# The value product of an attention stage: three passes per key tile against a half-empty stationary operand, or two passes against a full one, with the halves added afterwards

## What is computed

```python
for l in range(DEPTH):
    h = modulate(x, norm_mix_g[l], shift, scale)
    q, k, v = mixer_inputs(h, w_in[l], ...)      # 16 heads: 4 neighbourhood, 6 latent (MLA), 6 grouped (GQA)
    p = softmax(q @ k.T * scale + bias)          # latent queries: 512 latent + 128 cached context keys
    o = p @ v                                    # head dim 64
    x = x + gate_a * (concat(o) @ w_out[l])
    x = x + gate_f * swiglu(modulate(x, ...), w_gate[l], w_up[l], w_down[l])
```

## Time and profile before

| | before |
|---|---|
| runs, us | 1881.45, 1882.93, 1883.32 (median 1882.93) |
| profiled execution: its own time | 1889.33 us |
| its span in the profile | 1887.5 us |
| granted TensorE clock, mean | 0.956 of full |
| busy share PE, VectorE, ScalarE, GpSimd | 92%, 61%, 37%, 11% |
| attention stage, layer 0 | about 193 to 419 us of the span |
| attention stage, layer 1 | about 1105 to 1328 us of the span |

### The profile page before, as it was taken

How to read it: one execution, slowest core, us unless ns; L and a number is a source line. 1 busy time by engine, 2 the same in 40 slices (tenths; PEclk the granted TensorE clock), 3 DMA queues, 4 the chain that set the end, 5 groups by cost and what they waited for, 6 DMA issues and landing times.

```text
span 1887.5 us, 29279 instructions
## 1 busy us (share of the span) xinstructions
PE 1738.5 (92%) x11772; PEld 1684.5 (89%) x11772; DVE 1160.3 (61%) x2218; ACT 698.4 (37%) x1382; POOL 214.4 (11%) x314
## 2 busy tenths in 40 slices
PE   6899788889899999999989977899989999999997
PEld 6898677779899999999989966777889999999997
DVE  5997757873676777776652257788364444544444
ACT  2423755762522211222143366577253222112222
POOL 0001624320000000000010053523000000000001
PEclk9999879999899999999989988999989999999998
DMA  9573000014244343333122010000412222222201
GB/s 330 172 244 107 17 1 2 1 52 128 90 153 165 127 138 140 122 122 122 42 74 81 29 40 1 1 3 23 133 46 68 89 67 67 88 90 67 67 22 56
DMA packets 109561, 159.83 MB, mean 85 GB/s; under 512 B 5089, under 2 KB 87841, under 8 KB 109217
## 3 DMA queue, kind: packets, MB, share of 16 engines
q1 hardware_dynamic: 106672, 152.53, 24.3%
q0 software_dynamic: 640, 2.92, 0.6%
q10 hardware_dynamic: 2160, 3.23, 0.5%
HBM read 155.09 MB, written 3.57 MB: 84 GB/s over the span
## 4 chain that ended last, share of the span: by engine, by line
PE 77%; DVE 12%; ACT 4%; issue 2%; POOL 2%; DMA 2%; SPq 0%; POOLq 0%; DVEq 0%; ACTq 0%
PE ps L589 23%; PE ps L590 23%; PE ps L591 23%; DVE ps L1251 4%; PE ps L810 2%; PE ps L597 2%; DVE negmax L1456 1%; PE ps L789 1%; PE ps L653 1%; DVE K L1236 1%; DVE hT L1236 1%; PE ps L791 1%; DMA ada_n<-in_w_ada_first 1%; DMA wo_raw<-in_w_out 1%; DVE pT L1236 1%
## 5 line engine op out<-in xcount | busy, mean ns | idle before, releaser
L589 PE MATMUL ps<-hT,gw 128*128 128x320 f32 x1408 | 437.6, 311 | 6.8 <-DVE hT L1236 6.8
L590 PE MATMUL ps<-hT,gw 128*128 128x320 f32 x1408 | 437.3, 311 | 0.0
L591 PE MATMUL ps<-hT,gw 128*128 128x320 f32 x1408 | 437.2, 311 | 0.0
L1315 DVE SCALAR_TENSOR_TENSOR x<-ps,mod,x 128x320 f32<-128x320 f32 (+2 forms) x576 | 211.8, 433 | 120.1 <-PE ps L591 117.0
L589 PEld LDWEIGHTS ps<-hT,gw 128*128 128x128 f32 x1408 | 266.0, 189 | 7.3 <-issue 7.3
L590 PEld LDWEIGHTS ps<-hT,gw 128*128 128x128 f32 x1408 | 265.9, 189 | 0.0
L591 PEld LDWEIGHTS ps<-hT,gw 128*128 128x128 f32 x1408 | 265.8, 189 | 0.0
L1544 DVE TENSOR_TENSOR mm<-sl,ps 128x320 f32<-128x320 f32 x88 | 42.7, 487 | 318.1 <-issue 185.4
L589 PE MATMUL ps<-act,dw 128*128 128x320 f32 x704 | 219.3, 311 | 2.7 <-DVE act L1236 2.7
L590 PE MATMUL ps<-act,dw 128*128 128x320 f32 x704 | 219.0, 311 | 0.0
L591 PE MATMUL ps<-act,dw 128*128 128x320 f32 x704 | 218.9, 311 | 0.0
(11 more groups left out here) (201 smaller groups left out, 3644.3 us busy)
## 6 DMA issues: line engine op xcount, KB each, us to landing
gw_raw<-in_w_gate SPq DMA_DIRECT2D x22, 1024.0 KB, 5.5
gw_raw<-in_w_up SPq DMA_DIRECT2D x22, 1024.0 KB, 8.0
dw_raw<-in_w_down SPq DMA_DIRECT2D x22, 1024.0 KB, 5.0
ada_w<-in_w_adaT SPq DMA_DIRECT2D x39, 512.0 KB, 6.7
ada_wf<-in_w_adaT SPq DMA_DIRECT2D x34, 512.0 KB, 6.8
wi_raw<-in_w_in SPq DMA_DIRECT2D x16, 912.0 KB, 5.6
ada_wq<-in_w_adaT SPq DMA_DIRECT2D x19, 512.0 KB, 4.2
wo_raw<-in_w_out SPq DMA_DIRECT2D x16, 512.0 KB, 4.3
```

Source lines behind the costliest of these rows:

```text
L589: pe.matmul(dst, lh, rh, start=start, stop=False, skip_group_check=True)
L590: pe.matmul(dst, lh, rl, start=False, stop=False, skip_group_check=True)
L591: return pe.matmul(dst, ll, rh, start=False, stop=stop, skip_group_check=True)
L1315: i = ve.scalar_tensor_tensor(out=x[:, o, c0:c1], in0=ps[:, banks + hf_, s0:s0 + c1 - c0], scalar=mod[:, l, part * KD + o, q:q + 1], in1=x ...
```

## The change

V is laid out anew. For head A (slot 0) the stationary operand is [high | low], for head B [low | high], 128 full columns, with no zeros. Two passes are made with the same stationary operand, by pT high and by pT low. Partitions 0 to 63 of the bank then hold the product with one part of V and partitions 64 to 127 that with the other part, and the two halves must be added. (The fourth product, low by low, comes with them.) As each head now fills all partitions, the bank is emptied per head:

- `OL`, per head: ScalarE copies bank 6 to `o_raw` (semaphore `o_out`, which frees the bank for the next head). `OP`, per pair, directly behind `OF`: ScalarE copies both heads' context outputs from bank 7.
- SyncE moves one half of each head across partitions, in two DMAs of 64 x 640 elements, into `o_sum` (`o_moved`).
- `OA`, four slots after `OP`: GpSimd adds the other halves to it, in two instructions of 64 x 640 (`o_added`).
- `OH`, two slots later: ScalarE copies `o_sum` to the high part of `hT`. `OZ`, one slot later: GpSimd subtracts for the low part (`o_ready`).
- The last pair has no time for this. Head 14's half is moved by DMA and added by GpSimd (`OB`); the rest is copied across partitions by ScalarE and added by VectorE (`OA`, `OZ` of the last pair).
- The zeros and `vz_done` are gone. SyncE's program now has the moves ahead of the first two `wo_raw` loads.

```diff
@@ schedule()
         prompt = k >= 10 and k % 10 == 0
-        if k > 10 and k % 10 == 1:
-            order += [("OL", k // 10 - 1), ("OP", k // 10 - 1)]
         if prompt:
             order.append(("TP", k // 10 - 1))
         order += extra[2 * n]
         if 0 <= k < len(trans):
             order.append(trans[k])
+        if k >= 5 and k % 5 == 0:
+            order.append(("OL", k // 5 - 1))
         if prompt:
-            order.append(("OF", k // 10 - 1))
+            order += [("OF", k // 10 - 1), ("OP", k // 10 - 1)]
         order += extra[2 * n + 1]
-    order += [("OL", NP - 1), ("OP", NP - 1)]
+        for what, lag in (("OA", 4), ("OH", 6), ("OZ", 7)):
+            if k >= 10 and k % 10 == lag:
+                order.append((what, k // 10 - 1))
+    order += [("OA", NP - 1), ("OH", NP - 1), ("OZ", NP - 1)]
+    order.insert(order.index(("OL", NH - 1)), ("OB", NP - 1))
@@ SyncE, for s in SCHED
+                    if s[0] == "OP" and s[1] < NP - 1:
+                        pair = s[1]
+                        sp.wait_ge(o_out, l * 3 * NP + 3 * pair + 3)
+                        if pair or l:
+                            sp.wait_ge(o_ready, l * NP + pair)
+                        sp.dma_start(o_sum[0:64, :], o_raw[64:P, 0, :]).then_inc(o_moved, 16)
+                        sp.dma_start(o_sum[64:P, :], o_raw[0:64, 1, :]).then_inc(o_moved, 16)
+                    if s == ("OL", NH - 2):
+                        sp.wait_ge(o_out, l * 3 * NP + 3 * (NP - 1) + 1)
+                        sp.wait_ge(o_ready, l * NP + NP - 1)
+                        sp.dma_start(o_sum[0:64, 0:LAT], o_raw[64:P, 0, 0:LAT]).then_inc(o_moved, 16)
@@ TensorE, pv
-                                if pair > 0:
-                                    pe.wait_ge(o_ready, l * 2 * NP + 2 * pair - 1)
+                            if mt == 0 and g > 0:
+                                pe.wait_ge(o_out, l * 3 * NP + 3 * ((g - 1) // 2) + (g - 1) % 2 + 1)
                             pe.wait_ge(pT_ready, l * TS + n + 1)
...
-                            lh, ll = (V[:, pair % 2, q, vt, 64 * slot:64 * slot + P] for q in range(2))
-                            m = split_mm(ps[:, 6, c0:c1], lh, ll, pT_at(n, 0, c0, c1), pT_at(n, 1, c0, c1),
-                                         slot == 0 and mt == 0, False)
+                            for q in range(2):
+                                m = pe.matmul(ps[:, 6, c0:c1], V[:, pair % 2, vt, slot, :], pT_at(n, q, c0, c1),
+                                              start=mt == 0 and q == 0, stop=mt == 4 and q == 1, skip_group_check=True)
@@ TensorE, pvp: the same, with bank 7, and
-                            prev7[0] = (o_ready, 2 * NP, 2 * pair + 2)
+                            prev7[0] = (o_out, 3 * NP, 3 * pair + 3)
@@ ScalarE
-                sc.wait_ge(vz_done, l + 1)
...
+                            sc.activation(o_raw[:, g % 2, 0:LAT], ps[:, 6, :], ACT.Copy).then_inc(o_out, 1)
...
+                            sc.activation(o_raw[:, :, LAT:T], ps[:, 7, 0:2 * P].rearrange("p (a b) -> p a b", a=2),
+                                          ACT.Copy).then_inc(o_out, 1)
+                    elif s[0] == "OH":
+                        sc.wait_ge(o_added, l * 2 * NP + 2 * s[1] + 2)
+                        sc.activation(hT[:, PAIR_TILE[s[1]], 0, :], o_sum[:], ACT.Copy).then_inc(o_hi, 1)
@@ VectorE
-                    elif s[0] in ("OL", "OP"):
-                        o = PAIR_TILE[s[1]]
-                        part, bank, c0, c1 = (0, 6, 0, LAT) if s[0] == "OL" else (1, 7, LAT, T)
-                        ve.wait_ge(o_hi, l * 2 * NP + 2 * s[1] + part + 1)
-                        lo(hT[:, o, 1, c0:c1], ps[:, bank, 0:c1 - c0], hT[:, o, 0, c0:c1]).then_inc(o_ready, 1)
+                    elif s == ("OA", NP - 1):
+
+                        ve.wait_ge(o_out, l * 3 * NP + 3 * NP - 1)
+                        ve.tensor_tensor(o_sum[64:P, 0:LAT], ps[64:P, 6, :], o_sum[64:P, 0:LAT], ALU.add)
+                        ve.wait_ge(o_out, l * 3 * NP + 3 * NP)
+                        ve.tensor_tensor(o_sum[0:64, LAT:T], ps[0:64, 7, 0:P], o_sum[0:64, LAT:T], ALU.add)
+                        ve.tensor_tensor(o_sum[64:P, LAT:T], ps[64:P, 7, P:2 * P], o_sum[64:P, LAT:T], ALU.add).then_inc(o_added, 1)
+                    elif s == ("OZ", NP - 1):
+                        o_lo(ve, l, NP - 1)
@@ GpSimd
+                    elif s[0] == "OA" and s[1] < NP - 1:
+                        po.wait_ge(o_moved, 16 * (l * (2 * NP - 1) + 2 * s[1] + 2))
...
+                        for slot in range(2):
+                            r = slice(64 * slot, 64 * slot + 64)
+                            po.tensor_tensor(o_sum[r, :], o_raw[r, slot, :], o_sum[r, :], ALU.add).then_inc(o_added, 1)
+                            po.wait_ge(o_added, l * 2 * NP + 2 * s[1] + slot + 1)
+                    elif s[0] == "OB":
+                        po.wait_ge(o_moved, 16 * (l + 1) * (2 * NP - 1))
...
+                    elif s[0] == "OZ" and s[1] < NP - 1:
+                        o_lo(po, l, s[1])
```

More of the change, by code:

```diff
@@ L281, in build @@
         s5.close()
-        V = sb("V", [P, 2, 2, 6, 192], F32R)
+        V = sb("V", [P, 2, NT + 1, 2, P], F32R)
+        o_raw = sb("o_raw", [P, 2, T])
         K = sb("K", [P, 2, 2, KEYS], F32R)
@@ L466, in reciprocals, with o_lo @@
                 ve.reciprocal(rinv[:, w:w + 1], rsum[:, w:w + 1]).then_inc(rinv_ready, 1)
+        def o_lo(eng, l, pair):
+            eng.wait_ge(o_hi, l * NP + pair + 1)
+            o = PAIR_TILE[pair]
+            eng.tensor_tensor(hT[:, o, 1, :], o_sum[:], hT[:, o, 0, :].bitcast(F32), ALU.subtract).then_inc(o_ready, 1)
         def norm_unit(po, l, u):
@@ L844, in pvp @@
                             for slot in range(2):
-                                lh, ll = (V[:, pair % 2, q, 4, 64 * slot:64 * slot + P] for q in range(2))
                                 c0, c1 = slot * P, (slot + 1) * P
-                                m = split_mm(ps[:, 7, 0:P], lh, ll, pT_at(n, 0, c0, c1), pT_at(n, 1, c0, c1),
-                                             slot == 0, slot == 1)
+                                for q in range(2):
+                                    m = pe.matmul(ps[:, 7, c0:c1], V[:, pair % 2, 4, slot, :], pT_at(n, q, c0, c1),
+                                                  start=q == 0, stop=q == 1, skip_group_check=True)
                             m.then_inc(pv_done, 1)
-                            prev7[0] = (o_ready, 2 * NP, 2 * pair + 2)
+                            prev7[0] = (o_out, 3 * NP, 3 * pair + 3)
                         pending.append(pvp)
+                    elif s[0] == "OL" and s[1] == NH - 1:
+                        flush(1)
                     elif s[0] == "OF":
@@ L855, in _ @@
                         misc_step(l, *s[1:])
[L857 removed]
+                pe.wait_ge(o_ready, l * NP + NP)
                 for o in range(KD):
```

50 lines of the change are left out of this document (32 added, 18 removed).

## The result

The change made the kernel **slower by 1.0%**: 1903.72 us median (four runs, 1896.8 to 1905.91) against 1882.72 for the kernel before on the same chip, a ratio of 1.010 with a 95% interval of 1.0085 to 1.0115. The forecast of 1858 (1844 to 1877) had the sign wrong.

What follows compares the result with a forecast made beforehand. TensorE, busy 92% of the span, was taken as the main bound, with VectorE or several engines near full in some attention stretches. Stretch gains less a longer stage end gave 12.8 us a layer, 25.6 for two: 1858 us (1844 to 1877).

Steps and rivals of the forecast that it cites:

- One of three passes per key tile ... 18.6 us of TensorE work a layer: Value products of latent, grouped and neighbourhood heads: dropping one pass removes 18.6 us of TensorE work a layer at full clock.
- the fourth stretch: Latent heads, 312 to 340 us, TensorE full at full clock: 85% of 3.6 us credited, a gain of 3.1 us a layer.
- the second stretch: Neighbourhood heads, 236 to 278 us, clock 0.72: 80% of 2.5 plus 1.1 us credited, a gain of 2.9 us a layer.
- the clock as a rival: Grouped heads, 340 to 405 us: thinner work lets the clock fall to 0.72, total 1881 us, no change; chance 0.08.
- The wait at a pair's end shrinks ... I take 1.1 us a pair off: Pair ends: ScalarE alone frees banks 6 and 7, so TensorE's stand of 1.4 to 2.0 us becomes about 0.4.
- one more 512-column output per pair (0.60 us ...): ScalarE, each pair: one added copy of a 512-column output, 0.60 us, the next starting 0.47 us later.
- What hides GpSimd's 4.7 us is thus its own emptiness: Grouped heads: GpSimd's two additions and subtraction, 4.7 us a pair, are hidden, as it is busy 7.3 of 22.5 us.
- in the latent and grouped heads VectorE mostly reads one operand from PSUM: Latent and grouped heads: shared memory interfaces of GpSimd and VectorE would rarely contend, leaving the forecast sum as it is.
- ScalarE ... some 1.3 us a pair: ScalarE, each pair: the added 512-column copy and `OH` (640 columns, 0.74 us) together take some 1.3 us.
- The chain is 1.8 us longer: End of a layer's attention stage: pair 6's additions and the last pair's steps delay `o_ready`, costing 1.8 us a layer.
- The stall of `OH` at the rotary steps, 2.0 us: Stretch 278 to 312 us: a GpSimd rotation ahead of pair 1's additions delays `OH`; 2.0 us a layer, bounds 0 and 4.
- slower: `OH` holds ScalarE: Seven pairs a layer: late GpSimd additions make ScalarE wait 3 us before `OH`, exponentials behind it; 1899 us, chance 0.08.

Runs made afterwards that it cites:

- otherwise fast kernel: Three GpSimd additions of 128x640 with unused results for each of pairs 0 to 5, added to the kernel with two passes and pair-end copies one slot earlier: 1868.09 us.
- 1851.4 us: Kernel before with two passes and its pair-end copies to `hT` one slot earlier, ahead of the next exponential, without the new bookkeeping: 1851.42 us, ratio 0.9818.

## Why the prediction was wrong, step by step

**"One of three passes per key tile ... 18.6 us of TensorE work a layer."** The price of a pass was right at full clock: in the full latent pair TensorE's busy time falls by 2.5 us with two passes. Wrong was what came through. Two passes alone give 3 us, with the copies ahead 8.5 by the medians. In the fourth stretch, where TensorE was "full", I credited 85%, and 1.1 of 2.5 us came through even with the pair's end out of the way; what takes the rest was not isolated. In the second stretch I credited 80% and held the clock at 0.72. With less work in it the clock was lower, and the stretch got 2.7 to 3.8 us longer instead of shorter. A grouped pair gives 0.6 us (21.4 to 20.8). I had the clock as a rival for the grouped heads alone; the removed work costs time through it in the neighbourhood heads.

**"The wait at a pair's end shrinks ... I take 1.1 us a pair off."** Right in mechanism and too small: alone it gives 22 us, 1.6 for each of 14 pair ends. Part of that is clock: the second stretch of layer 0 ran at 0.71 before and at 0.90 with this edit alone, and in the kernels with two passes the edit takes 15.6 us off TensorE's busy time (1718.2 to 1702.6) for the same instructions, of 28.8 us in all. I had taken the gain for a property of the new layout. It only needs the old copies one slot earlier.

**What failed most: the even head's copy.** The prediction had the added copy as "one more 512-column output per pair (0.60 us ...)", busy time alone. It never asked where that copy stands against the product that it waits for. At the pair's end `TP` and `OF` push the pending products out; at an even head nothing does, so ScalarE stands up to a slot, an exponential and the next scores stand behind it, and at times the clock falls behind them. That is 17 us (1903.7 against 1886.9 with this copy alone moved), some 7 of them clock. The order listing ahead of the prediction showed a pair's end only; the even head's end should have stood there too.

**"What hides GpSimd's 4.7 us is thus its own emptiness."** Each added instruction was sized rightly (64x640 took 1554 ns at the median, 1.6 predicted), and GpSimd was idle, but VectorE wasn't: its instructions with two operands in memory took up to 1.4 us longer when they began beside GpSimd's additions. I had cited the Trainium skill's rule on shared interfaces (GPSIMD Engine Reference, Specifications) and wrote that "in the latent and grouped heads VectorE mostly reads one operand from PSUM". Mostly, but for four instructions into V a pair and one or so into K, and V's are made in the very slot of `OZ`. As many microseconds of GpSimd work in an otherwise fast kernel cost 16.7 us. In the changed kernel only part of these meet (V's instructions take 7.9 us in a layer against 5.3 before). Moving `OZ` away from them gave some 10 us (3 to 17) with the even heads' copy as it was, and nothing once that copy was later; so its price in the changed kernel is not a fixed one.

**"ScalarE ... some 1.3 us a pair."** The size is right (0.60 and 0.737 us); it costs 8.0 us in all (by the medians) where it can be seen.

**"The chain is 1.8 us longer."** It is 3.7 a layer. Half was missed: in the drain, head 14's copy-out stands for pair 6's additions and holds the transposed copies behind it, first GpSimd's row, then ScalarE's, then TensorE's:

```profile
412.56 3.16 POOL L1720 TENSOR_TENSOR o_sum<-o_raw,o_sum 64x640 f32<-64x640 f32 x2
```

```profile
415.82 0.60 ACT L1177 ACTIVATE o_raw<-ps 128x512 f32<-128x512 f32 x1 [2.38 <-POOL o_sum L1720]
```

```profile
416.47 0.73 PE L852 MATMUL ps<-pT,V 128*128 128x512 f32 x2 [1.59 <-ACT o_raw L1177]
```

**The stall of `OH` at the rotary steps, 2.0 us.** It didn't occur: the trace shows ScalarE standing before `OH` for the last pair alone. The rival "slower: `OH` holds ScalarE" gave 1899, near the result, and had the right kind of cause (ScalarE in order before a step of the bookkeeping, exponentials behind it) at the wrong step.

**The clock.** I gave it 0.08 and looked for it in the grouped heads. There it fell in one stretch of three in layer 0 (0.93, 26.0 us against 22.2 before) and in none of layer 1; most of its falls lie in the neighbourhood and latent stretches.

**A balance.** From 1851.4 us: 16.9 for the even heads' copy, 16.7 for GpSimd's work, 8.0 for ScalarE's, and about 4 a layer for the longer end beyond what GpSimd's work already adds to it (25.3 against 20.0, of which 1.1), 8.4 in all: 1901.4, against 1903.7 measured. Each was measured in another kernel, in differences of medians that are uncertain by up to 9 us each, and several didn't add up when combined, so the agreement is no proof and may be luck; it says only that no further large cost is needed.

## What to carry to other kernels

For every instruction that an in-order engine gets, find in the other engine's program the instruction that it waits for, and see how much stands between; a product kept pending for pipelining is later than the list of steps says. Before removing work from the busiest engine, move the copy that frees its bank: here one step moved by a slot gave 22 us, and with it the shorter product paid more, for 1851.4 us in all. One variant, flushing the pending product at an even head's end too, was not tried.

An idle engine is not a free one if a busy one waits for it: here its work has to be priced by VectorE's instructions with two operands in memory that fall beside it. And a mean clock read from a stretch is no constant to cost work at: less work, or one pause more, can change it.

## What the runs showed of the hardware

An addition on GpSimd takes as long on 64 partitions (1554 ns for 640 columns) as the subtraction `OZ` on 128 (1550 ns). The VectorE instruction on V with two operands in memory (128x320) takes 0.48 us alone and 1.35 us when it begins 0.5 us into a GpSimd subtraction of 1.54 us, and its end keeps 0.34 to 0.36 us behind GpSimd's; `pT`, with one operand in a bank, stays at 0.68 us. A move of 160 KB between partitions landed 2.6 us after its issue. The granted clock fell behind some short pauses of TensorE (1.46 us in the place shown) inside stretches that were otherwise full, and not behind others (the same pause of 1.46 us in layer 1, or one of 2.70 us before 287.72), so that the same program took 31.2 us in one layer and 38.0 in the other. Less work in a stretch with pauses went with a lower clock: 0.90 with three passes, 0.78 with two.
